# Output projection of tile 0: attention heads paired two to a chunk, so that each w_out chunk is 128 consecutive rows

## What is computed

```
h = modulate(x_prompt, mod_p[:, 0], mod_p[:, 1], g_norm1)
q, kvc_p, kvs_p, kvw_p, gates, u_p = mix_inputs(h, w_in, g_qnorm, g_knorm)
o_nsa = nsa_prompt(q, gates, kvc_p, kvs_p, kvw_p, cmp_pe, w_cmp, g_knorm, slopes)
o_pool = pool_mix(u_p, ...)
x1 = x_prompt + mod_p[:, 2][:, None, :] * mix_out(o_nsa, o_pool, w_out)
h2 = modulate(x1, mod_p[:, 3], mod_p[:, 4], g_norm2)
y_prompt = x1 + mod_p[:, 5][:, None, :] * peer(h2, peer_wq, peer_subkeys, peer_u, peer_v)

def mix_out(o_nsa, o_pool, w_out):
    return jnp.concatenate([o_nsa.reshape(B, T, NSA_W), o_pool], axis=-1) @ w_out
```

## Time and profile before

| | |
|---|---|
| median of 3 runs | 2571.34 us (2564.22, 2571.34, 2575.87) |
| span of the profiled execution | 2572.8 us |
| time of the profiled execution outside its span | none is recorded |
| PE matmul busy | 1280.7 us, 50% |
| DVE busy | 1757.6 us, 68% |
| POOL busy | 1184.3 us, 46% |
| ACT busy | 212.5 us, 8% |
| HBM read and written over the span | 368 GB/s |

### The profile page before, as it was taken

One profiled execution on the slowest core, in us unless ns is written; L12 is line 12 of the kernel. 1 busy time (PEld: TensorE's weight loads), 2 busy tenths in 40 slices (PEclk: granted clock), 3 DMA queues, 4 the chain that ended last, 5 costly groups with the idle time before them and its releaser, 6 DMA issues.

```text
span 2572.8 us, 17754 instructions
## 1 busy us (share of the span) xinstructions
PE 1280.7 (50%) x6315; PEld 697.2 (27%) x6317; DVE 1757.6 (68%) x2243; ACT 212.5 (8%) x559; POOL 1184.3 (46%) x686
## 2 busy tenths in 40 slices
PE   5699998897490543266884972000015655200000
PEld 2363534482240432143331960000002222000000
DVE  1010112217967977897557667999999998899898
ACT  3110012100001221121001010000000000000000
POOL 1000100002426744575222415678876767788684
PEclk9799898899795655556995985555556677655555
DMA  9949899659999999999998989999999999999897
GB/s 299 332 172 422 324 414 291 208 196 360 388 422 397 377 366 341 405 410 370 344 373 321 414 318 410 366 393 422 422 407 407 400 420 417 417 422 422 366 422 307
DMA packets 163042, 944.49 MB, mean 367 GB/s; under 512 B 34635, under 2 KB 44435, under 8 KB 56830
## 3 DMA queue, kind: packets, MB, share of 16 engines
q0 software_dynamic: 94784, 682.66, 66.0%
q1 hardware_dynamic: 68175, 260.74, 28.2%
HBM read 937.36 MB, written 10.26 MB: 368 GB/s over the span
## 4 chain that ended last, share of the span: by engine, by line
PE 27%; DMA 25%; DVE 20%; POOL 15%; issue 9%; SPq 2%; ACT 1%; POOLq 0%; another core or an unknown queue 0%; DVEq 0%; ACTq 0%
POOL arena L668 11%; DMA arena<-in_peer_u,arena 10%; DMA arena<-in_peer_v,arena 9%; DVE arena L1975 8%; POOL arena L680 4%; DVE arena L1998 4%; DMA arena<-in_w_out 4%; PE PS L1468 3%; PE PS L1445 3%; PE PS L1016 3%; DMA arena<-in_w_ada 3%; PE PS L1166 2%; PE PS L1253 2%; PE PS L966 2%; PE PS L1423 2%
## 5 line engine op out<-in xcount | busy, mean ns | idle before, releaser
L668 POOL DMA_INDIRECT arena<-in_peer_u,arena x256 | 471.7, 1843 | 446.1 <-DVE arena L1975 240.8
L1975 DVE CUSTOM_DVE_ANT_0 arena<-arena 128x2048 f32<-128x2048 f32 x256 | 581.5, 2289 | 118.0 <-DMA arena<-in_peer_u,arena 116.7
L1998 DVE SCALAR_TENSOR_TENSOR arena<-arena 128x2048 f32<-128x2048 f32 x226 | 531.1, 2350 | 136.6 <-DMA arena<-in_peer_v,arena 131.9
L668 POOL DMA_INDIRECT arena<-in_peer_v,arena x256 | 428.3, 1673 | 369.7 <-DVE arena L1998 242.7
L1468 PE MATMUL PS<-arena 128*128 128x512 f32 x240 | 180.3, 921 | 449.9 <-DMA arena<-in_peer_v,arena 449.9
L1468 PEld LDWEIGHTS PS<-arena 128*128 128x128 f32 x240 | 69.5, 304 | 561.4 <-issue 555.1
L1474 PE MATMUL PS<-arena 128*64 128x512 f32 x8 | 5.5, 849 | 346.4 <-DVEq L2041 346.4
L2031 DVE SCALAR_TENSOR_TENSOR arena<-arena 128x2048 f32<-128x2048 f32 x64 | 150.6, 2352 | 10.8 <-DMA arena<-in_peer_v,arena 5.3
L966 PE MATMUL PS<-arena 128*32 128x512 f32 x768 | 119.4, 721 | 69.9 <-DMA arena<-in_w_ada 66.6
L2028 DVE CUSTOM_DVE_ANT_0 arena<-arena 128x2048 f32<-128x2048 f32 x64 | 145.0, 2291 | 8.4 <-DMA arena<-in_peer_u,arena 6.5
L680 POOL DMA_INDIRECT arena<-in_peer_v,arena x64 | 126.4, 1975 | 39.0 <-issue 18.6
(11 more groups left out here) (347 smaller groups left out, 1824.5 us busy)
## 6 DMA issues: line engine op xcount, KB each, us to landing
arena<-in_w_ada SPq DMA_DIRECT2D x96, 1024.0 KB, 12.1
arena<-in_w_in SPq DMA_DIRECT2D x32, 1048.0 KB, 9.2
arena<-in_peer_wq SPq DMA_DIRECT2D x32, 1024.0 KB, 10.2
arena<-in_w_in SPq DMA_DIRECT2D x32, 768.0 KB, 11.2
arena<-in_w_out SPq DMA_DIRECT2D x16, 1024.0 KB, 30.0
arena<-in_w_out SPq DMA_DIRECT2D x32, 512.0 KB, 24.0
arena<-in_peer_u,arena POOLq DMA_INDIRECT x320, 13.9
arena<-in_peer_v,arena POOLq DMA_INDIRECT x320, 15.5
```

The lines of the kernel that those rows point to most:

```text
L668: pool.indirect_dma_start(out=rows_ring[:, k % NROW, :], out_offset=None, in_=tables[kind], in_offset=bass.IndirectOffsetOnAxis(ap=ids[:, ...
L1975: V.tensor_tensor_reduce(out=buf, in0=buf, in1=h2(t), scale=1.0, scalar=0.0, op0=ALU.mult, op1=ALU.add, accum_out=dots[:, t, r:r + 1]).the ...
L1998: V.scalar_tensor_tensor(out=acc[t], in0=rows_ring[:, k % NROW, :], scalar=dots[:, t, r:r + 1], in1=acc[t], op0=ALU.mult, op1=ALU.add).the ...
```

## The change

Two neighbouring heads (2k and 2k + 1) now share a chunk, so that each of chunks 0 to 7 is 128 consecutive rows of w_out and comes in one transfer.

- **Transfers.** All 16 pieces of tile 0's w_out are issued by one line, 128 partitions each. The order of the list follows the new order of use.
- **Where a unit's output goes.** Heads r and r + 1 of one key group come from two units, 2k and 2k + 1. An even unit's two heads go to partitions 0 to 63, an odd unit's to 64 to 127; gi = 0 uses columns 256 to 383 of bank 7 and gi = 1 columns 384 to 511. All 6 matmuls of a unit therefore have one `tile_position`, and they are sorted so that the three of gi = 0 come first. ScalarE's copy takes 64 partitions by 256 columns in place of 128 by 128, into two chunks of `OT0`.
- **When a chunk can be used.** A pair of units completes two chunks, so TensorE takes the chunks of the heads in the order 0, 2, 1, 3, 4, 6, 5, 7, the first of them in unit 2 in place of unit 1; two are left for after unit 7 in place of one. Each waits for both units of its pair.

```diff
-        POOL_FIRST = [8, 0, 9, 10, 1, 11, 2, 12, 3, 13, 4, 14, 5, 15, 6, 7]
+        PAIR_ORDER = [0, 2, 1, 3, 4, 6, 5, 7]
+        OUT_ORDER = [8, 9] + [c for k in range(6) for c in (10 + k, PAIR_ORDER[k])] + PAIR_ORDER[6:]
...
-            elif kind == "out" and n >= 8:
+            elif kind == "out":
                 eng.dma_start(dst[:, 0:D], I["w_out"][rows_of(n), :]).then_inc(done, 16)
-            elif kind == "out":
-                for gi in range(2):
-                    eng.dma_start(dst[64 * gi:64 * gi + 64, 0:D], w_out_nsa[n // 4, gi, :, n % 4, :]).then_inc(done, 16)
...
                 act.wait_ge(s_o, u + 1)
-                A(OT0[:, u, :], PS[:, 7, 256:384], copy).then_inc(s_oc, 1)
+                gp, half = u // 4, slice(64 * (u % 2), 64 * (u % 2) + 64)
+                c = 4 * gp + u % 4 // 2
+                A(OT0[half, c:c + 3:2, :], PS[half, 7, 256:512].rearrange("p (a b) -> p a b", a=2), copy).then_inc(s_oc, 1)
...
                     w = need("out", c)
-                    wait(pe, s_oc, c + 1 if c < 8 else 0)
+                    wait(pe, s_oc, 2 * (PAIR_ORDER.index(c) // 2) + 2 if c < 8 else 0)
...
                     if u == 1:
                         pe.wait_ge(s_gb, 4)
-                        out0(8, 0)
+                        out0(8)
                     out0(8 + u)
...
-                for rhs, lhs, gi, k in steps:
-                    last = mm(PS[64 * gi:64 * gi + 64, 7, 256:384], lhs, rhs, start=(k == 0), stop=(k == 2), tile_position=(0, 64 * gi))
+                for rhs, lhs, gi, k in sorted(steps, key=lambda step: step[2:]):
+                    last = mm(PS[64 * (r % 2):64 * (r % 2) + 64, 7, 256 + gi * 128:384 + gi * 128], lhs, rhs, start=(k == 0), stop=(k == 2), tile_position=(0, 64 * (r % 2)))
                 last.then_inc(s_o, 1)
                 if u > 1:
-                    out0(u - 1)
-            out0(7)
+                    out0(PAIR_ORDER[u - 2])
+            out0(*PAIR_ORDER[6:])
```

More of the change, by code:

```diff
@@ L368, in build @@
         pieces += [("ada", 4, c) for c in range(NK)]
-        pieces += [("out", c) for c in POOL_FIRST]
+        pieces += [("out", c) for c in OUT_ORDER]
         n_wq0 = len(pieces)
@@ L397, in build @@
             k = slot_number(i)
-            count[k % 12] += 32 if p[0] == "out" and p[1] < 8 or p[0] == "out1" and p[2] < 4 else 16
+            count[k % 12] += 32 if p[0] == "out1" and p[2] < 4 else 16
             arrived.append(count[k % 12])
```

## The result

The changed kernel takes 2576.84 us (median of 20 runs, 2573.14 to 2584.15), the kernel before 2568.90 us (20 runs, 2562.82 to 2575.87): ratio 1.0031, 95% interval 1.002 to 1.0041, so 5 to 11 us slower, about 8 us by the medians. The forecast of 2575 us held within 2 us and the loss is under 0.5%, as forecast, but the loss of 3.4 us was less than half of the one measured. That the total came so near is in part luck: the three runs of the kernel before that it started from had a median of 2571.34 us, 2.4 us above that of the 20.

A forecast was written before the change was run, and what follows sets the result against it. It took TensorE's own work to bound tile 0's projection. Terms of 0.55, 0.47 and 2.34 us made 3.4 us on a 2572.8 us span, 2576.2; less 1.5 us for the profiled execution, about 2575 us, range 2563 to 2586.

The forecast's parts named there:

- the loss of 3.4 us: Forecast total for tile 0's projection: unit 0 0.55 us, unit 1 0.47, units 2 to 7 2.34; chance 0.74 for 1 to 7 us.
- What bounds the stage: Tile 0's projection: TensorE's own work sets the time, with w_out's transfers wholly hidden behind it by about 4 us.
- Transfers, 0: Whole w_out transfers in tile 0 cost and gain 0 on the path, with 1.4 us as the bound on the gain.
- The rival of 37 us: Tile 0's transfers were really the bound, so whole ones save up to 37 us, giving 2534 us; chance 0.04.
- Values' products, 0.39 us a unit: TensorE's 12 passes a unit, all in one half, go from 0.95 to 1.34 us, 0.39 us more.
- Its factor of two: Estimate from the skill page: a unit's products go from 0.95 to 1.90 us, the eight units costing 7.6 us.
- ScalarE's copy, 0.08 us: Copying 256 columns in place of 128 takes 0.08 us more, showing only after units 0 and 1.
- The moved chunk and the pairs, 0: Chunk 0's passes go from unit 1 to behind unit 7; the count stays 128 and no new wait forms.
- All of it reaches the end: Behind tile 0's projection a late start isn't made good, so the whole 3.4 us reach the kernel's end.
- The draining rival: Values' passes in one half drain between passes: 2.33 us more a unit, 18.6 us in all, 2590 us; chance 0.08.
- The forecast's 3.1 to 3.4 us: Tile 0's projection ends this much later, the lower figure if TensorE's clock rises at the same moment as before.

The follow-up runs named there:

- run 1: Changed kernel with chunks 0 to 7 of tile 0's w_out again in two transfers of 64 partitions each: 2574.18 us, ratio 1.0018 to the kernel before.
- run 2: Kernel before with only tile 0's w_out transfers made whole, 128 consecutive rows each, heads' rows mismatched: 2568.97 us, ratio 0.9996.
- run 9: Kernel before with heads paired in all three tiles, two units' products at once and every w_out transfer whole: 2544.67 us, ratio 0.9908.
- run 10: Kernel before with heads paired and w_out transfers whole in tiles 1 and 2 only, tile 0 untouched: 2544.24 us, ratio 0.99.
- run 7: Kernel before with only the w_out transfers of tiles 1 and 2 made whole, rows meeting the wrong heads: 2544.23 us, ratio 0.9899.
- run 4: Changed kernel with a unit's products alternating between gi = 0's and gi = 1's columns, in one half, one start and stop: 2574.44 us, ratio 1.0021.
- run 8: Changed kernel with both 15-row products first, then gi = 0's and gi = 1's 128-row ones, one start and stop: 2572.25 us, one execution.
- run 3: Kernel before with only the order of a unit's six products changed, gi = 0's three first, each in its own half: 2576.79 us, ratio 1.0033.
- run 6: Changed kernel with two units' products done together, alternating between the column halves, and one copy for both: 2570.98 us, ratio 0.9998 to the kernel before.
- run 5: Kernel before with each unit's values' products done four times over, as a known delay on TensorE: 2592.70 us, ratio 1.0093.

## Why the prediction was right, and where it was wrong

**What bounds the stage: right.** TensorE alone. (I had read it as busy without a gap from 416 us on; from 420 to 480 us it is busy 59.53 of 60 us, since the wait for L782 falls there.) w_out's waits on the page belong to tiles 1 and 2. Runs 1, 2 and 9 against 10 show it from both sides, and run 7 shows the 1% that such transfers are worth where the chain does wait for them.

**Transfers, 0: right.** Run 2 measured 0.9996, run 1 the changed kernel's stage to 0.01 us. The rival of 37 us had only the DMA share and the equal pace for it.

**Values' products, 0.39 us a unit: this is the step that failed.** "So 12 x 0.112 = 1.34 us, 0.39 us more per unit": measured 0.93 us. The kind of cost was right, its size was 2.4 times too small. The pace of one pass, 0.112 us, was nearly right: 0.109 us. But the sum set bare passes, 12 x 0.112 us, against a measured 0.95 us that holds changes of shape too. Twelve passes in one half are 1.31 us; the 1.59 us of runs 4 and 8 hold 0.28 us more, 0.14 us at the change of row count inside and 0.14 us at the two ends, where the products meet matmuls of another shape. In the kernel before, six pairs at 0.109 us are 0.65 us, and the same changes make it 0.95. So the lost overlap is 0.64 us (0.95 to 1.59 us), the whole gain that the halves gave. The other 0.29 us are the two further changes that sorting by gi brings in, a term that the sum did not have; L1253 has no change of shape, so its pace could show neither. The Trainium skill (TensorEngine Tiling (Array Packing), Key Properties) states that a change of tiling mode drains the engine; the 0.14 us agree, if a product of 15 rows and one of 128 differ in mode, which no run here shows by itself. Its factor of two, which I had noted beside the sum as 7.6 us, holds for the bare passes (0.109 us for two in different halves, 0.109 us for one alone). That 7.6 us is so near the 7.4 us measured is luck: the overlap is 8 x 0.64 = 5.1 us of it, the extra changes are the rest.

**ScalarE's copy, 0.08 us: right within 0.02.** It takes 0.378 us against 0.277. It shows after units 0 and 1 only: TensorE waited for it twice, 1.1 us in all, the longest 0.6 us.

**The moved chunk and the pairs, 0: right.** Run 3 has the whole loss without them, run 6 has them without the loss.

**All of it reaches the end: right.** Run 5: 22.9 us put in, 21 us out, with an interval of 19 to 29 us.

**The sum with the measured term.** Units 2 to 7, at full clock in both profiles: 487.38 − 428.32 = 59.06 us before; after, 492.51 − 424.46 = 68.05 us, less 3.43 us for the moved chunk (10.51 us for three chunks at the end, 7.08 us for two in the kernel before), so 5.56 us for six units, 0.93 us each. Eight make 7.4 us, and with 0.2 us for the copies 7.6, where 5 to 11 us was measured. The draining rival, 2.33 us a unit, is excluded.

**Why the profiles' stages differed by 3.5 us.** The kernel before had TensorE at half clock until about 418 us in its one profile, the changed one until about 407 us. Run 2, the same program but for the transfers, was at full clock from 405 us and took 82.04 us where the kernel before took 85.88. Its chain answers to the earlier trace rows:

```profile
400.74 1.93 PE PS L963 x8
...
411.80 10.50 PE PS L1163 x24
422.30 0.98 PE PS L1223 x12
...
482.78 2.50 DVE PS L1800 x4
```

From unit 1's products to the end both took 60.48 us (487.38 − 426.90 and 482.78 − 422.30), so the whole 3.84 us lie in front of them, where the one was at half clock for longer; the same 24 passes took 10.50 us here and 11.98 us there. It isn't the transfers: run 10, whose tile 0 is wholly that of the kernel before, was at full clock from 407 us too. Against run 2 the changed kernel's stage is 7.3 us longer (each was at half clock for the first 4.3 us of it), which is the products' loss. The forecast's 3.1 to 3.4 us had taken this clock as given for both.

## What to carry to other kernels

A high DMA share is no bound: look whether any engine waits for those bytes, and in which stage, before making transfers wider; here the same kind of edit was worth nothing in tile 0 and 1% in tiles 1 and 2. A new layout must keep alternating between the halves of the array and group products of equal row count; price it by matmuls with the same changes of shape, not by the pace of a uniform run. Two profiles that differ in granted clock can hide a loss, so compare stages with a run that has only one part of the change.

## What the runs showed of the hardware

Two matmuls of 64 columns in different halves overlap fully: two passes start every 0.109 us, where one half takes one (12 passes in 0.95 us against 1.59 us, changes of shape included); accumulating into the same columns in a row costs nothing (1.59 us in runs 4 and 8 alike); a change between operands of 15 and 128 rows costs 0.14 us, in either direction. With a part of the pieces in transfers of 64 partitions the DMA engines are at a share of 1.01 and move 252 GB/s (run 1), where whole ones alone need 0.59 for 210 GB/s (the changed kernel). When TensorE's clock rises again after the waits for w_ada differs between executions of nearly the same program: it was at 0.50 until about 418 us in the kernel before, until 405 us in run 2 and 407 us in run 10, and in run 3 it never fell in this stage. What decides it stays open; its worth was about 4 us here.
